# A hybrid streaming-encoder trunk in float32: values of two chunks in one go, outputs of chunks 4 and 5 rounded ahead of the last maxima, exponentials ahead of the copy in odd chunks

## The reference

```python
h = rmsnorm(x, attn_norm_g[l])
proj = h @ w_in[l]
q, k, v, conv_in, gate_logits = jnp.split(proj, SPLITS, axis=-1)
...
y_attn = sliding_window_sink_attention(q, k, v, attn_sinks[l]) @ w_attn_o[l]
u = ca * jax.nn.sigmoid(cb)
u = causal_dwconv(u, conv_dw_w[l], conv_dw_b[l])
u = jax.nn.silu(layernorm(u, conv_ln_g[l], conv_ln_b[l]))
y_conv = u @ w_conv_o[l]
merged = jax.nn.sigmoid(g_attn) * y_attn + jax.nn.sigmoid(g_conv) * y_conv
x = x + merged @ w_out[l]
h = rmsnorm(x, ffn_norm_g[l])
up = causal_dwconv(h @ w_ffn_up[l], ffn_dw_w[l], ffn_dw_b[l])
gt, val = jnp.split(up, 2, axis=-1)
x = x + (jax.nn.silu(gt) * val) @ w_ffn_down[l]
```

```python
s = jnp.einsum('bcqkgd,bcjkd->bckgqj', qc, kb).astype(jnp.float32) * scale
m = jnp.maximum(jnp.max(s, axis=-1, keepdims=True), sink)
p = jnp.exp(s - m)
denom = jnp.sum(p, axis=-1, keepdims=True) + jnp.exp(sink - m)
probs = (p / denom).astype(v.dtype)
o = jnp.einsum('bckgqj,bcjkd->bcqkgd', probs, vb)
```

## Time and profile before

| | |
|---|---|
| median of 3 runs | 798.37 us (798.12 to 798.52) |
| the profiled execution | 798.24 us |
| its span in the trace | 796.4 us |
| TensorE matmuls (PE) busy | 787.8 us, 99% |
| weight loads (PEld) busy | 718.0 us, 90% |
| ScalarE (ACT), VectorE (DVE), GpSimd (POOL) busy | 69%, 65%, 82% |
| DMA, HBM read | 140.68 MB, 178 GB/s over the span |

### The profile page before, as it was taken

How to read it: one execution, slowest core, us unless ns; L and a number is a source line. 1 busy time by engine, 2 the same in 40 slices (tenths; PEclk the granted TensorE clock), 3 DMA queues, 4 the chain that set the end, 5 groups by cost and what they waited for, 6 DMA issues and landing times.

```text
span 796.4 us, 14013 instructions
## 1 busy us (share of the span) xinstructions
PE 787.8 (99%) x5470; PEld 718.0 (90%) x5470; DVE 520.3 (65%) x1186; ACT 547.5 (69%) x924; POOL 649.6 (82%) x182
## 2 busy tenths in 40 slices
PE   8999999999999999999999999999999999999997
PEld 8999989899988888888899999999899888888885
DVE  6899999674656666631359999885545666666101
ACT  7868978765676776763456577887546776767932
POOL 6999778787878888898869987878788888888982
PEclk9999999999999999999999999999999999999999
DMA  8655434444545555455454544434464555455631
GB/s 305 235 188 206 159 113 154 160 165 161 204 166 204 184 187 195 175 211 211 168 200 169 199 155 164 142 131 159 159 238 166 186 178 208 167 207 172 223 134 54
DMA packets 21378, 142.63 MB, mean 179 GB/s; under 512 B 2496, under 2 KB 3008, under 8 KB 4672
## 3 DMA queue, kind: packets, MB, share of 16 engines
q1 hardware_dynamic: 20736, 140.69, 49.9%
q10 hardware_dynamic: 576, 1.04, 0.4%
HBM read 140.68 MB, written 1.05 MB: 178 GB/s over the span
## 4 chain that ended last, share of the span: by engine, by line
PE 93%; DVE 3%; ACT 2%; DMA 1%; issue 0%; SPq 0%; DVEq 0%; ACTq 0%
PE four L1379 26%; PE four L1386 13%; PE four L1128 12%; PE four L1130 11%; PE four L1129 11%; PE four L1460 5%; PE four L1482 3%; PE four L1481 3%; PE four L1480 3%; PE four L1464 2%; DVE pc L817 2%; PE four L1262 1%; DMA x<-in_x_t 1%; PE ps L1240 1%; PE pt L1251 1%; ACT whi L345 1%
## 5 line engine op out<-in xcount | busy, mean ns | idle before, releaser
L288 POOL TENSOR_TENSOR wlo<-raw,whi 128x2048 fp32r<-128x2048 f32 x128 | 591.5, 4626 | 124.7 <-ACT whi L345 124.4
L345 ACT ACTIVATE whi<-raw 128x2048 fp32r<-128x2048 f32 x129 | 247.0, 1915 | 52.0 <-PE four L1464 27.4
L1379 PE MATMUL four<-u_both,whi 128*128 128x512 f32 x800 | 201.8, 392 | 0.0
L1128 PE MATMUL four<-h_both,whi 128*128 128x256 f32 x608 | 174.2, 286 | 0.0
L1130 PE MATMUL four<-h_both,wlo 128*128 128x256 f32 x608 | 172.0, 283 | 0.0
L1129 PE MATMUL four<-h_both,whi 128*128 128x256 f32 x608 | 172.0, 283 | 0.0
L1379 PEld LDWEIGHTS four<-u_both,whi 128*128 128x128 f32 x800 | 143.3, 189 | 25.1
L817 DVE SCALAR_TENSOR_TENSOR pc<-upad,par_all,pc 128x256 f32<-128x256 f32 x404 | 162.9, 481 | 0.1
L1128 PEld LDWEIGHTS four<-h_both,whi 128*128 128x128 f32 x608 | 116.5, 192 | 5.2 <-issue 5.2
L1386 PEld LDWEIGHTS four<-u_both,wlo 128*128 128x128 f32 x800 | 110.2, 190 | 8.6
L1129 PEld LDWEIGHTS four<-h_both,whi 128*128 128x128 f32 x608 | 116.6, 192 | 0.0
(11 more groups left out here) (278 smaller groups left out, 1242.8 us busy)
## 6 DMA issues: line engine op xcount, KB each, us to landing
raw<-in_weights SPq DMA_DIRECT2D x130, 1024.0 KB, 4.8
raw<-in_weights SPq DMA_DIRECT2D x3, 512.0 KB, 8.0
out_y<-qk SPq DMA_DIRECT2D x3, 256.0 KB, 2.4
x<-in_x_t SPq DMA_DIRECT2D x2, 256.0 KB, 3.9
raw<-in_weights SPq DMA_DIRECT2D x2, 256.0 KB, 3.9
x<-in_x_t SPq DMA_DIRECT2D x1, 512.0 KB, 6.9
gate<-in_final_g ACTq DMA_DIRECT2D x1, 512.0 KB, 3.7
out_y<-qk ACTq DMA_DIRECT2D x1, 256.0 KB, 3.0
```

The source lines that it names most:

```text
L288: nc.gpsimd.tensor_tensor(wlo[s][:, :], raw[s][:, :], whi[s][:, :].bitcast(f32), ALU.subtract).then_inc(lo_ready[s], 1)
L345: A(whi[s][:, :], raw[s][:, :], ACT.Copy).then_inc(hi_ready[s], 1)
L1128: MM(out, whi[s][:, w], hi, start=start, stop=False, skip_group_check=accumulate)
L1379: MM(to[:, m, :, :].rearrange("p a t -> p (a t)"), whi[u % RING][:, w], both[:, k, :, :].rearrange("p a t -> p (a t)"), start=(k == 0), st ...
```

## The change

`po` is now used in both halves: the output of an even n goes to the first, that of an odd n to the second. TensorE issues `values` of 0 and 1, of 2 and 3, of 4 and 5 one behind the other, after the units U_GATE+3, +5 and +7 and ahead of the transposes of 2, 4 and 6; `pv_done` counts two at the end of such a pair. `values(6)` and `values(7)` stay where they were. ScalarE copies both outputs of a pair with one instruction (`high_of_both`), VectorE subtracts both with one (`low_of_both`). The pairs 0, 1 and 2, 3 are copied in steps 3 and 5; the pair 4, 5 in step 6 on ScalarE, behind the probabilities of 6, and in step 7 on VectorE, ahead of the maxima of 7. In odd steps ScalarE does the exponentials ahead of the eviction.

```diff
-        outputs = po[:, 0, :].rearrange("p (b t) -> p b t", b=GROUP_PAIRS)
+        outputs = [po[:, a, :].rearrange("p (b t) -> p b t", b=GROUP_PAIRS) for a in range(2)]
+
+        output_pair = po[:, :, :].rearrange("p a (b t) -> p a b t", b=GROUP_PAIRS)
...
+                def high_of_both(n):
+
+                    c, g = n % N_CHUNKS, n // N_CHUNKS
+                    act.wait_ge(pv_done, l * GROUPS + n + 2)
+                    both = oh[:, 4 * g:4 * g + 4, CHUNK * c:CHUNK * c + 2 * CHUNK].rearrange("p b (a t) -> p a b t", a=2)
+                    A(both, output_pair, ACT.Copy).then_inc(oh_ready, 2)
...
                 for i in range(NT):
                     u = U_GATE + i
-                    if i >= 1:
+                    if i % 2 == 0 and i:
                         evict_transposed(i - 1)
                     if l > 0 or i > 1:
                         exps(i)
                     elif i == 0:
                         exps(0)
                         exps(1)
-                    if i >= 2:
-                        high_of_o(i - 2)
+                    if i % 2:
+                        evict_transposed(i - 1)
+                    if i in (3, 5):
+                        high_of_both(i - 3)
                     probabilities(i)
+                    if i == GROUPS - 2:
+                        high_of_both(i - 2)
...
+                def low_of_both(n):
+
+                    c, g = n % N_CHUNKS, n // N_CHUNKS
+                    dve.wait_ge(oh_ready, l * GROUPS + n + 2)
+                    at = (slice(0, P), slice(4 * g, 4 * g + 4), slice(CHUNK * c, CHUNK * c + 2 * CHUNK))
+                    high, low = [half[at].rearrange("p b (a t) -> p a b t", a=2) for half in (oh, ol)]
+                    V.tensor_tensor(low, output_pair, high.bitcast(f32), ALU.subtract).then_inc(ol_ready, 2)
...
+                    if i == GROUPS - 1:
+                        low_of_both(i - 3)
                     maxima(i)
                     conv(step_now, step_now + taps[0])
                     denominators(i)
-                    if i >= 2:
-                        low_of_o(i - 2)
+                    if i in (3, 5):
+                        low_of_both(i - 3)
                     conv(step_now + taps[0], step_now + sum(taps))
...
-                    if n:
+                    if n and (n % 2 == 0 or n == GROUPS - 1):
                         pe.wait_ge(ol_ready, l * GROUPS + n)
...
-                    last.then_inc(pv_done, 1)
+                    if n >= GROUPS - 2:
+                        last.then_inc(pv_done, 1)
+                    elif n % 2:
+                        last.then_inc(pv_done, 2)
...
                     if i == GROUPS - 1:
                         values(i - 1)
+                    elif i and i % 2 == 0:
+                        values(i - 2)
+                        values(i - 1)
                     transpose_probs(i)
-                    if 0 < i < GROUPS - 1:
-                        values(i - 1)
```

More of the change, by code:

```diff
@@ L518, in high_of_o @@
                     act.wait_ge(pv_done, l * GROUPS + n + 1)
-                    A(oh[:, 4 * g:4 * g + 4, CHUNK * c:CHUNK * c + CHUNK], outputs, ACT.Copy).then_inc(oh_ready, 1)
+                    A(oh[:, 4 * g:4 * g + 4, CHUNK * c:CHUNK * c + CHUNK], outputs[n % 2], ACT.Copy).then_inc(oh_ready, 1)
+                def high_of_both(n):
[3 more added lines that the diff above has]
+                    A(both, output_pair, ACT.Copy).then_inc(oh_ready, 2)
                 def exps(n):
@@ L892, in low_of_o @@
                     at = (slice(0, P), slice(4 * g, 4 * g + 4), slice(CHUNK * c, CHUNK * c + CHUNK))
-                    V.tensor_tensor(ol[at], outputs, oh[at].bitcast(f32), ALU.subtract).then_inc(ol_ready, 1)
+                    V.tensor_tensor(ol[at], outputs[n % 2], oh[at].bitcast(f32), ALU.subtract).then_inc(ol_ready, 1)
+                def low_of_both(n):
[4 more added lines that the diff above has]
+                    V.tensor_tensor(low, output_pair, high.bitcast(f32), ALU.subtract).then_inc(ol_ready, 2)
                 dve.wait_ge(par_ready, l * 5 + 5)
@@ L1261, in values @@
                         rows, queries = slice(64 * odd, 64 * odd + 64), slice(CHUNK * (odd ^ (n % 2)), CHUNK * (odd ^ (n % 2)) + CHUNK)
-                        last = MM(outputs[rows, :, :], vwin[:, c, HEAD_DIM * g:HEAD_DIM * g + HEAD_DIM],
+                        last = MM(outputs[n % 2][rows, :, :], vwin[:, c, HEAD_DIM * g:HEAD_DIM * g + HEAD_DIM],
                                   probsT[n % 2][:, :, queries], start=True, stop=True)
-                    last.then_inc(pv_done, 1)
+                    if n >= GROUPS - 2:
+                        last.then_inc(pv_done, 1)
+                    elif n % 2:
+                        last.then_inc(pv_done, 2)
                 def convolved(p):
```

## The result

| | before | after |
|---|---|---|
| median of the runs, us | 798.46 (5 runs, 798.12 to 798.67) | 807.11 (5 runs, 805.2 to 807.51) |
| ratio, after to before | | 1.0103, 95% interval 1.0092 to 1.0113 |
| profiled execution, its span, us | 798.24, 796.4 | 805.2, 803.4 |
| mean granted clock of the runs | 0.998 to 1.0 | 0.994 in one, 0.992 in one, 0.990 in three |

The account below looks back on a forecast made before the run. TensorE, busy 99% of the 796.4 us span, was taken as the bound. Terms -2.2 - 0.1 + 6.9 = +4.6 us on the profiled 798.24 gave 802.8 us, range 801.4 to 804.6.

Parts of the forecast that it names:

- edit 3: Merged copy of outputs 4 and 5, behind chunk 6's probabilities on ScalarE: TensorE waits 3.44 us a layer, +6.9 us.
- T: The four transposes of a chunk on TensorE, between two weight units; alone they were priced at 0.44 us.
- The sum of 8.73: ScalarE's way from the start of unit U_GATE+7's last product to chunk 7's transposes: 8.73 us.
- V: A chunk's values product on TensorE; 0.58 us until the transposes start, 0.46 if right behind another values product.
- edit 1: Values products issued in pairs on TensorE: saves 0.36 us a pair, three pairs a layer, two layers, -2.2 us.
- The rival with 0.58: Second values product costs 0.58, not 0.46 us; each pair saves 0.24, total 803.5 us; inside the forecast's case, no separate chance.
- the wait of 3.44: TensorE's wait per layer up to chunk 7's transposes: ScalarE's way of 8.73 us against TensorE's own 5.29.
- edit 2: Exponentials ahead of the eviction in odd chunks: shortens the wait before chunk 4's scores in layer 0, -0.1 us.
- GpSimd and VectorE hidden: Behind the merged copy: GpSimd's low half of U_AO+1 hidden by 0.25 us; VectorE's 4.2 us at most within ScalarE's 5.1.
- The clock falls: Rival: in the gap TensorE's clock drops to 1.2 GHz for 24 products, 2.9 us a layer, 808.6 us; chance 0.05.
- The case: The forecast's own case: wait less savings, +4.6 us, 802.8 us, range 801.4 to 804.6; chance 0.86.
- Nothing takes it back: After the stage nothing on TensorE's path waits for another engine, so the delay of +4.6 us remains.

Follow-up runs that it names:

- the clock held up: The changed kernel with 20 unused matmuls of 256 columns added ahead of the values product of chunk 6: 803.25 us, ratio 1.0058.
- the later four runs: The changed kernel itself, unedited, run again in a second series: 804.92 us (804.29 to 805.85), ratio 1.0085.

## Why the prediction was wrong, point by point

- **The wait, edit 3: right, in place and size.** From the start of the unit's last product to the merged copy I had 1.35 us; it was 1.40 (140.53 to 141.93). From there to T of chunk 7 I had 3.96 + 3.42 = 7.38; it was 7.34 (to 149.27). The sum of 8.73 came out as 8.74. Idle before V 6 was 2.79 for about 2.7, before T 7 0.29 and 0.53 for about 0.8, ScalarE's idle time 2.38 for 2 to 3.
- **The pairs, edit 1: right.** V, V, T cost 1.60 us (140.53 to 142.37, less 0.24) for 1.62. The eight matmuls of a pair take 1.08 to the end of the last, 0.43 more than one V, close to the 0.46 of a V without a way in and out. The rival with 0.58 is out. The Trainium skill, page "TensorEngine Tiling (Array Packing)", section "Key Properties", says that a change of tiling mode, and not just of the tile, drains TensorE; this row, 0.43 us for a second V in the same mode, agrees.
- **Both together: right.** T of chunk 7 starts 2.30 us later in layer 0 (149.27 for 146.97), where the terms give 2.26: the wait of 3.44 less 3 x 0.36 for the pairs and 0.1 for edit 2. In layer 1 it starts 5.61 later (543.97 for 538.36): 2.30, the 1.04 that the clock took in layer 0, and 2.27. With the clock held up the kernel stood 4.7 us above before, for 4.6.
- **GpSimd and VectorE hidden: right.** The low half of U_AO+1 ended at 149.42, 8.89 us after the last product as forecast, and before U_AO+1's first product at 150.03; no wait for VectorE or GpSimd shows in the stage.
- **Edit 2: right as a net, incomplete as a mechanism.** The wait before the scores of chunk 4 went from 0.4 to 0.3. But I looked at the scores alone. The eviction's new place also hides the round trip to VectorE's denominators, worth up to 0.5 us a layer as soon as chunk 7's probabilities are what TensorE waits for. And the 8.73 was right here by luck: I listed chunk 7's eviction in the queue and gave it no term. The 2.02 from first exponential to first probability, read from before, holds a copy (0.39) and 0.17 of idle time that are no longer there, and the eviction took just their place: 145.90 to 147.93 is 2.03.
- **The clock: wrong, and this is the step that failed.** I had named the rival "The clock falls", with the right mechanism and the right place, and gave it 0.05 because "the gap is short and broken". My sum put the clock at nothing, with no row behind that: it rested on the absence of a fall in a kernel without such a gap. A gap of 2.79 us, alone or with V and 0.53 more behind it, was enough in three of the four layers traced. The size in the rival, 2.9 us a layer, was too large: a fall cost 1.0 to 1.4 us in the trace, since the products stepped by 0.21 and not 0.24 and the full clock was back 3.4 us after the fall, before the 24 of them were through. The median carries 3.9 us of it, more than the 2.4 of the traced execution, and between my 0 and the rival's 5.8. In the later four runs it is 1.7 us, and their 804.92 lies only 0.3 above my range: how far the range was missed is in part chance, that it was missed is not.
- **The range was wrong for the same reason.** It was spread by hand-overs that proved good to 0.1 us, and took in nothing of the one mechanism that no row of before could price. Since the change was the first thing to put such a gap into this kernel, the absence of a fall in the earlier trace rows said nothing on what a gap does. The trace of before does hold one fall, which I had not looked for: in its last 0.5 us, 5.0 us after TensorE's last matmul. The case should have had a much larger chance and the range its reach, to 808.6.
- **Nothing takes it back: right.** In the trace V of chunk 7 in layer 1 starts 7.05 us late (548.93 for 541.88), and the span is 7.0 us longer.

**Still open.** The three slowest runs of the change (0.990) were not traced. Two falls of 1.0 and 1.4 us explain the profiled 805.2, not the 807.3. An estimate: 3.4 us at half clock lower the mean over 803 us by 0.002, so 0.990 instead of 0.994 asks for about two falls more, and at 1.2 us each these give 807.6. The fall at 12 us in another kernel's trace shows that there are other places for one, and two of the 75 runs of the kernel before lie at 800.1 and 800.2 us with a mean clock of 0.997, which would fit one fall there; where the slowest runs had theirs I can't say. Nor did the runs settle why the same waits lowered the clock in one layer and not in the other. The ends of the programs show the same scatter: in the 13 traces the clock fell 2.1 to 5.0 us after TensorE's last matmul. What sets the moment stays open.

## What to carry to other kernels

- Before merging or moving a copy on a helper engine, list what is queued behind it there and measure from the event it waits for to the instruction that the bottleneck needs; here that one sum gave the wait to 0.1 us. An instruction that waits late should stand behind the urgent ones, or where its input is long done.
- If a change puts the first idle gap of some microseconds into a busy TensorE, price the clock's fall as a likely case, and look for it in stretches of 1 to 3 us, and in the mean clock of each run: a profile page with slices of 20 us shows full clock throughout.
- When one wait is removed, the next entry of the same queue is the candidate for the new one; moving the tap products cost 2.2 us until the copy behind them was moved as well, and with both moved the kernel was as fast as without either, or 0.5 us faster, which these runs can't tell.

## What the runs showed of the hardware

- TensorE's granted clock fell to 1.2 GHz behind an idle time of 2.79 us, once within the V that followed and twice within the T behind V and 0.53 us more; and behind 1.86 us and a V, within the next wait or soon after it. It did not fall with 0.47 and 0.54 around the V, nor in the stage of the kernel whose longest wait there was 1.2 us. But in one trace it fell at 12.3 us behind waits of 1.35 and 0.24 us, so these figures are no safe limits. Each of these six falls lasted 3.4 us. At the ends of the programs, where nothing follows, the clock fell between 2.1 us (the copy first in step 7) and 5.0 us (before) after the last matmul. The Trainium skill, page "TensorE: Matmul & The Clock Gate", Part 1, says that an idle TensorE is put back to the lower level; the trace agrees, and here it took less idle time than I had thought a risk.
- The fall is not a fixed property of the program: with the same waits it came in both layers of one traced execution and in one layer of another, and the change's nine runs spread from 804.3 to 807.5 us in step with their mean clock, while the kernels without the gap stay mostly within 1 us of each other.
- At half clock the products stepped by 0.21 us where the full clock has 0.12: less than twice.
